# Two moves in a two-layer decoder kernel's hand-written order: VectorE's table doublings, and two GpSimd masks

## The reference, cut to what matters

```
h = rms_norm(x);  proj = h @ w_in
A: S5 state space, 32 groups, 64 complex states:  s[t] = a * s[t-1] + B u[t];  y = Re(C s) + d*u;  gelu, glu
B: native sparse attention (compressed, selected and window branches)
C: stick-breaking attention:  w = where(key < query, exp(log_sigmoid(z) + after), 0);  out = w @ v
x = x + (sum over branches of sigmoid gate * (branch @ w_branch)) @ w_out
x = x + conv_ffn(rms_norm(x))
```

## Time and profile before

| | us |
|---|---|
| median of 3 runs | 993.47 (993.08 to 993.66) |
| the profiled execution's own time | 991.46 |
| its span, first to last instruction | 989.7 |
| TensorE busy | 953.2 (96%) |
| VectorE busy | 746.2 (75%) |
| ScalarE busy | 565.4 (57%) |
| GpSimd busy | 338.2 (34%) |
| HBM traffic, mean | 158 GB/s |
| chain that ended last | TensorE 73%, VectorE 16%, ScalarE 5%, issue 3%, GpSimd 2%, DMA 1% |

### The profile page before, as it was taken

One profiled execution on the slowest core, in us unless ns is written; L12 is line 12 of the kernel. 1 busy time (PEld: TensorE's weight loads), 2 busy tenths in 40 slices (PEclk: granted clock), 3 DMA queues, 4 the chain that ended last, 5 costly groups with the idle time before them and its releaser, 6 DMA issues.

```text
span 989.7 us, 17232 instructions
## 1 busy us (share of the span) xinstructions
PE 953.2 (96%) x6447; PEld 819.5 (83%) x6447; DVE 746.2 (75%) x1240; ACT 565.4 (57%) x905; POOL 338.2 (34%) x267
## 2 busy tenths in 40 slices
PE   7899899999999999999999998999999999999997
PEld 6799666776878999999989986777777799999996
DVE  5989999995666776677865689999857676665666
ACT  6436665757454655555564466666664555555544
POOL 0111666671320563155401047568506001011010
PEclk9999999999999999999999999999999999999999
DMA  8963433344554765555468424233645345655551
GB/s 230 263 187 96 133 114 128 122 98 164 168 168 136 204 196 179 181 200 170 132 179 255 155 93 128 85 129 103 183 141 170 128 152 190 200 182 177 200 176 43
DMA packets 135864, 156.83 MB, mean 158 GB/s; under 512 B 16400, under 2 KB 103032, under 8 KB 135800
## 3 DMA queue, kind: packets, MB, share of 16 engines
q1 hardware_dynamic: 135800, 155.98, 50.7%
HBM read 154.92 MB, written 1.05 MB: 158 GB/s over the span
## 4 chain that ended last, share of the span: by engine, by line
PE 73%; DVE 16%; ACT 5%; issue 3%; POOL 2%; DMA 1%; SPq 0%; DVEq 0%; ACTq 0%; POOLq 0%; PEldq 0%
PE pj L736 52%; PE bX L736 6%; PE bA L736 5%; DVE wl L1556 5%; PE bB L736 4%; PE bY L1085 2%; DVE s5x L1885 1%; PE bY L736 1%; DVE work L1849 1%; DVE bnat L1885 1%; POOL s5h L2144 1%; PE bX L1074 1%; DVE gate L1572 1%; DVE hl L1578 1%; PE bO L736 1%
## 5 line engine op out<-in xcount | busy, mean ns | idle before, releaser
L1556 DVE TENSOR_TENSOR wl<-ring,wh 128x1024 fp32r<-128x1024 f32 (+1 forms) x276 | 365.0, 1326 | 136.4 <-ACT wh L1262 134.9
L1262 ACT ACTIVATE wh<-ring 128x1024 fp32r<-128x1024 f32 (+1 forms) x276 | 289.0, 1048 | 238.2 <-PE pj L736 201.4
L736 PE MATMUL pj<-hh,wh 128*128 128x256 f32 x1024 | 293.1, 286 | 6.7 <-DVE wl L1556 4.8
L736 PE MATMUL pj<-hl,wh 128*128 128x256 f32 x1024 | 289.7, 283 | 0.0
L736 PE MATMUL pj<-hh,wl 128*128 128x256 f32 x1024 | 289.7, 283 | 0.0
L736 PEld LDWEIGHTS pj<-hh,wh 128*128 128x128 f32 x1024 | 196.2, 192 | 11.3 <-issue 6.6
L736 PEld LDWEIGHTS pj<-hl,wh 128*128 128x128 f32 x1024 | 196.3, 192 | 1.2 <-issue 0.5
L736 PEld LDWEIGHTS pj<-hh,wl 128*128 128x128 f32 x1024 | 196.3, 192 | 0.0
L736 PE MATMUL pj<-wh,hl 128*128 128x512 f32 (+1 forms) x416 | 169.3, 407 | 10.3 <-ACT sbv L1249 4.9
L736 PE MATMUL pj<-wh,hh 128*128 128x512 f32 (+1 forms) x416 | 160.5, 386 | 0.0
L736 PE MATMUL pj<-wl,hh 128*128 128x512 f32 (+1 forms) x416 | 159.9, 384 | 0.0
(11 more groups left out here) (315 smaller groups left out, 1473.7 us busy)
## 6 DMA issues: line engine op xcount, KB each, us to landing
ring<-in_ffn_w_up SPq DMA_DIRECT2D x44, 1024.0 KB, 5.1
ring<-in_w_in SPq DMA_DIRECT2D x40, 1024.0 KB, 5.2
ring<-in_ffn_w_down SPq DMA_DIRECT2D x22, 1024.0 KB, 4.9
ring<-in_w_in SPq DMA_DIRECT2D x16, 512.0 KB, 5.3
ring<-in_w_branch SPq DMA_DIRECT2D x8, 1024.0 KB, 5.1
ring<-in_w_out SPq DMA_DIRECT2D x8, 1024.0 KB, 5.1
ring<-in_w_branch SPq DMA_DIRECT2D x8, 512.0 KB, 5.8
ring<-in_w_in SPq DMA_DIRECT2D x8, 256.0 KB, 5.1
```

The lines of the kernel that those rows point to most:

```text
L736: return nc.tensor.matmul(o, a, b, start=start, stop=stop, skip_group_check=True)
L1262: A(dst, src, ACT.Copy).then_inc(w_hi.sem, 1)
L1556: TT(dst, src, hi.bitcast(F32), ALU.subtract).then_inc(w_lo.sem, 1)
```

## The change

In `TABLE` the doublings 5 and 6 of tiles 0 to 3 are now in slots 1 and 2, those of tiles 4 to 9 in slots 5 and 6 (before: 0 and 1), those of tiles 10 to 15 in slots 8 and 10 (before: 2 and 3). `s5_b` is in slot 0. `table_ends` runs after each group of tiles, in slots 2, 6 and 10. In both layers the mask of pair 0's weights is in slot 29 instead of 28, and that of pair 1's in slot 32, ahead of the last `s5_back`, instead of 33.

```diff
-SB_D = {s - (k == 0): k for s, k in SB_M.items()}
+SB_D = {s - (k == 1): k for s, k in SB_M.items()}
...
-TABLE = {0: (4, 10, 5, 6), 1: (4, 10, 6, 7), 2: (10, ST, 5, 6), 3: (10, ST, 6, 7)}
+TABLE = {1: (0, 4, 5, 6), 2: (0, 4, 6, 7), 5: (4, 10, 5, 6), 6: (4, 10, 6, 7), 8: (10, ST, 5, 6), 10: (10, ST, 6, 7)}
...
                 split_lo(l, 8)
-                if l == 0:
-                    table(tmp_d, 0, 4, 5, 6)
                 split_lo(l, 9)
-                if l == 0:
-                    table(tmp_d, 0, 4, 6, 7)
                 split_lo(l, 10)
-                if l == 0:
-                    s5_b()
-                for s in range(11, 13):
+                for s in range(11, 14):
                     split_lo(l, s)
-
-                split_lo(l, 13)
...
-                def table_ends():
+                def table_ends(lo=0, hi=ST):
                     for n, (src, sign) in enumerate(((0, 1.0), (1, 1.0), (1, -1.0), (0, 1.0))):
-                        ins = TS(ends[:, :, n], tab[:, src, :, P - 1], sign, None, ALU.mult)
+                        ins = TS(ends[:, lo:hi, n], tab[:, src, lo:hi, P - 1], sign, None, ALU.mult)
                     stepped(ins)
...
+                    if l == 0 and q == 0:
+                        s5_b()
                     if l == 0 and q in TABLE:
                         table(tmp_d, *TABLE[q])
-                        if q == max(TABLE):
-                            table_ends()
+                        lo, hi, _, last = TABLE[q]
+                        if last == 7:
+                            table_ends(lo, hi)
```

## The result

| | before | after |
|---|---|---|
| median of the runs, us | 993.28 | 1004.0 |
| ratio, 95% interval | | 1.0117 [1.0104, 1.0129] |
| profiled execution, us | 991.46 | 1006.86 |
| its mean granted clock | 0.997 | 0.984 |
| TensorE busy | 953.2 (96%) | 961.6 (96%) |

The change costs 10.7 us. The profiled execution is the slowest of its four; the others took 1002.6 to 1004.3 us. So the two profiles stand 15.4 us apart while the medians stand 10.7 apart, and what makes that difference is itself a finding: see experiment 12 and the account of the sum.

A forecast was written before the change was run, and what follows sets the result against it. VectorE's full queue behind the reduction, ahead of TensorE's slot 12, was taken to bind. -1.35 + 10.7 - 1.0 + 1.0 + 1.6 - 2.1 = +8.9 us, giving 1002.4 us on the median; range 997.5 to 1006.5.

The forecast's parts named there:

- Ahead of the slots: Before layer one's slots: VectorE loses 7.20 us of work, TensorE gains only its piece 11 wait, -1.35 us (bounds 0 and -1.35).
- Slots 0 to 4: 7.20 us of table work replaces 9.83 on VectorE, which had 1.77 us to spare; nothing is paid.
- Slots 5 to 10: Table work on VectorE's full stretch delays pair 2's maximum and slot 12: +10.7 us, less 1.0 for a filled wait.
- Sharing with GpSimd: Doublings in slots 5 to 10 stretched beside GpSimd, mostly a swap: +1 us, bounds 0 and 4.
- Where TensorE pays: TensorE held up at slots 9 to 11, then an `sbv` wait at slot 12 near 6 us, ending near 131.
- The clock: Slot 12's multiplications slow down behind the longer wait: one loss of +1.6 us, bounds 0 and 3.2.
- The masks: Pair 1's values start earlier in both layers, partly limited by ScalarE's gate copy: -2.1 us, bounds 0 and -3.2.
- The sum: All terms together: +8.9 us, 1000.4 for the profiled execution, 1002.4 on the median; bounds 998.7 and 1007.0.
- the first: Rival: VectorE is full but not binding, the 10.7 us hide, -3.5 us in all: 990.0; chance 0.12.
- the second: Rival: half of the 10.7 us is absorbed around slots 9 to 12 or later, +3.5: 997.0; chance 0.15.
- the third: Rival: the masks bring nothing because ScalarE's copies pace slots 35 and up, +11.0: 1004.5; chance 0.12.
- the fourth: Rival: work removed ahead of the slots brings nothing, the DMA taking its place, +1.35: 1003.8; chance inside the forecast's bounds.

The follow-up runs named there:

- experiment 12: `after_again`: the changed kernel run once more, unchanged, in the third series; 1003.99 us, ratio 1.0112 to the kernel before.
- early_only: Kernel before with `s5_b` and tiles 0 to 3's doublings moved into slots 0 to 2, tiles 4 to 15's last two doublings left out; 990.34 us, 0.9982.
- after_warm: Changed kernel with small unread multiplications filling TensorE's waits ahead of slots 8 and 12 (layer one) and 12 (layer two); 1002.22 us, 1.0097.
- tables_only: Changed kernel with the old mask slots put back, so all of the table edit alone; 1005.46 us, 1.0126 to the kernel before.
- half_late: Changed kernel with masks as before and tiles 4 to 9's doublings in slots 3 and 4 instead of 5 and 6; 1002.75 us, 1.0102.
- copy_first: Changed kernel with ScalarE's `sbk` and `sbv` copies moved ahead of the attention work in slots 7 and 11, both layers; 1000.26 us, 1.007.
- masks_only: Kernel before with the two weight masks moved and nothing else; 991.43 us, 0.9994.
- masks_warm: Kernel before with both masks moved and nine small multiplications ahead of slot 12 in each layer; 988.38 us, 0.9957.
- late_only: Kernel before with only tiles 4 to 15's doublings moved, to slots 5, 6, 8 and 10, and `table_ends` as in the change; 1007.3 us, 1.0149.
- slot3: As `half_late`, but both doublings of tiles 4 to 9 in slot 3 instead of slots 3 and 4; 1000.99 us, 1.008.

## Why the prediction was right

It gave 1002.4 us, and 1004.0 were measured. By its own steps:

- **Ahead of the slots, -1.35.** TensorE's waits for low parts fell from four to three, as the prediction said. The reduction moved by 1.02 in the first profile, by 1.84 in `early_only` and by 2.17 in `after_again`. The size is right on the mean: in the seven traces that have this edit (`after`, `after_again`, `after_warm`, `tables_only`, `early_only`, `half_late`, `copy_first`) the reduction stands at 87.91 to 89.06, mean 88.62, in the four without it (`before`, `masks_only`, `masks_warm`, `late_only`) at 89.92 to 90.50, mean 90.16, so 1.5 us. The bound of 1.35 was too tight, and its reason (no more idle time of TensorE) did not hold: the waits for low parts fell from 4.8 us to 3.6, 3.3 and 2.9 in these three, so the ones left shrank too. Why executions of the same program differ here is open.
- **Slots 0 to 4, nothing.** Right: 4.26 us of VectorE's room are left with the new work in it. That the room ends at the reduction is what `half_late` and `slot3` show. The prediction took this reduction for slot 5's; it is slot 4's. That changed nothing here, since the change puts no work in slot 4, but it was the mistake of `half_late`.
- **Slots 5 to 10, +10.7 less 1.0.** Right to 0.1 us: 10.66 and 1.01.
- **Sharing with GpSimd, +1.** This was the mis-sized term: 3.1 us net in the profile. I took most places for a swap, and only about half of the 6.4 us gross was one. The 128x384 doublings of slots 6 and 10 lost about 1.07 us on each of two instructions (1.62 and 1.61 against 0.55). The 3.1 us are within the stated bound of 4. That the partner is GpSimd's turn back is read from the rows side by side; no run took GpSimd's work away from there. The Trainium skill (SBUF — State Buffer, section "SBUF: two separate sides") says that the loser blocks for the other's whole instruction; the prediction put its price at 2 us for slot 10's doubling, and the trace agrees: 5.22 less 3.05 is 2.17, and slot 6's lost 2.11 as well. Weighing that rule more than the row of one low part would have brought the sum nearer.
- **Where TensorE pays.** Only half seen. The prediction named slots 9 to 12 and one wait near 6 us that ends near 131. There are two, 8.1 us at slot 8 and 4.4 at slot 12, ending at 134.71. The maximum of pair 2 came at 131.47, not near 128; the 3.5 us between are the sharing (2.1), new waits (1.25), for which the sum had no term, and the smaller gain in front (0.3). The first of these waits comes from slot 6's block by way of ScalarE's queue in slot 7, which I had not read.
- **The clock, +1.6.** Within its bounds or just past them. In the first profile it was 3.4: slot 12 took 2.5 us longer than before in layer one and 0.9 longer in layer two. In `after_again` it was 0.9: 2.5 longer in layer one, 1.56 shorter in layer two. Such a loss at slot 12 can be 2.5 us and not only the 1.6 that the prediction took for one. The half clock from 106 to 120 us cost almost nothing at slot 12, since `after_warm` has none of it and starts slot 12 only 0.16 us nearer to the reduction.
- **The masks, -2.1.** -1.65 by `masks_only`'s chains and -1.74 by the profile after. Right in mechanism: the gain is 1.69 at the values and is cut by ScalarE's gate copy, and also by the wait of 0.30 for the state output, which the prediction had ruled out. The medians alone (-0.6, interval -1.6 to +0.4) would not have shown it.
- **The sum.** For the profiled execution it gave 1000.4, and that took 1006.86; another took 1003.24. On the medians it is 1.6 us low. Part of its accuracy is luck: from the reduction to slot 12 the price was 14.0 us where the sum had 10.7, and in the median something that the sum did not hold made up for most of it. Its upper bound (1007.0) also kept the masks' -2.1 although their own bound was 0. Typical executions of the kernel before, at 993, seem to lose more to the clock than the profiled one at 991.46 did: `masks_warm` takes 988.38, and only about 1.7 of those 4.5 us are the masks'. The runs' mean clocks point the same way: in the three series the kernel before took 991.2 to 992.2 us in the 14 runs with a mean granted clock of 0.997, the profiled one's, and 992.5 to 994.0 in the 31 runs at 0.995 or 0.996. The distance of the groups' medians, 991.75 and 993.15, is near one loss of 1.6 at a slot 12. If so, the new losses replace old ones in part. No execution of the slower group was profiled, so where it loses is argued, not shown.
- **The rivals.** VectorE binds (`late_only`, 14.5 us), so the first falls. Nothing is absorbed: the lag is 15.66 us behind slot 12 and still 15.70 at 216.10, ahead of the masks; so the second falls. The masks bring 1.65 by the chains, so the third falls, and the removed work brings 1.5, so the fourth does.

## What to carry to other kernels

An engine's total says nothing about where its work is free. Find two instances of the same schedule, here two layers, one with the work and one without, and compare their waits: the work is free up to the last wait that only shrank (here the reduction of slot 4, with 4.3 us of room), and costs its full length behind it. When work goes into a full queue, follow every item behind it, not only the last: a third engine whose queue has a consumer of it ahead of a PSUM copy stops TensorE there. And price a block that will run beside GpSimd at its stretched duration, instruction by instruction.

## What was not expected of the hardware

Nine small multiplications in a wait of 2.4 us, in each layer, were worth more than the moved masks: 991.43 to 988.38 us between `masks_only` and `masks_warm` (of two series, whose medians of the kernel before differ by 0.1). Without them, slot 12 of layer two took 4.54 us, with them 2.96, and the runs of one series spread over 0.4 us (five runs) instead of 4.2 (eleven). The Trainium skill (TensorE: Matmul & The Clock Gate, section "Why this matters for your kernels") warns of idle gaps between bursts of matmuls. The waits of 2.4 us here are shorter than the gaps for which it gives the fall, and behind them the clock was down in some executions and layers and up in others (the earlier trace rows has one of each), so here the measurement goes further than the page. The fill was tried only together with the masks, not in the kernel before.

VectorE's small operations suffer beside GpSimd too: sixteen of 64x120 went from 3.83 to 8.64 us. So work given to GpSimd in a stretch where it has nothing to do is not free: VectorE paid for it in both runs that tried.
